# Band attention's values as one pair of weight blocks with seven products, its weight sums written in place

## The reference, cut to what matters

```python
def chunk_band_attention(h, w_qkv, q_g, k_g, rel_bias):
    qkv = (h @ w_qkv).reshape(bsz, seq, 3, C_HEADS, C_HEAD_DIM)
    q = rmsnorm(qkv[:, :, 0], q_g) * (C_HEAD_DIM ** -0.5)
    k = rmsnorm(qkv[:, :, 1], k_g)
    v = qkv[:, :, 2]
    ...
        s = jnp.einsum('bqhd,bkhd->bhqk', q_c, k_b).astype(jnp.float32) + bias
        s = jnp.where(valid, s, -jnp.inf)
        prob = jax.nn.softmax(s, -1).astype(v.dtype)
        return jnp.einsum('bhqk,bkhd->bqhd', prob, v_b)
```

## Time and profile before

| what | value |
|---|---|
| time, median of 3 runs | 2069.96 us (2067.13 to 2071.61) |
| the profiled execution | 2068.74 us, its span 2067.0 us |
| TensorE busy | 2025.5 us, 98% of the span |
| VectorE busy | 1172.6 us, 57% |
| ScalarE busy | 403.8 us, 20% |
| mean granted TensorE clock | 0.993 of full speed |

### The profile page before, as it was taken

One profiled execution on the slowest core, in us unless ns is written; L12 is line 12 of the kernel. 1 busy time (PEld: TensorE's weight loads), 2 busy tenths in 40 slices (PEclk: granted clock), 3 DMA queues, 4 the chain that ended last, 5 costly groups with the idle time before them and its releaser, 6 DMA issues.

```text
span 2067.0 us, 24997 instructions
## 1 busy us (share of the span) xinstructions
PE 2025.5 (98%) x10844; PEld 1439.1 (70%) x10844; DVE 1172.6 (57%) x1651; ACT 403.8 (20%) x831; POOL 10.7 (1%) x22
## 2 busy tenths in 40 slices
PE   8999999999999999999999999999999999999998
PEld 7886766984486599446864556988884466659973
DVE  4664784754463475544434854455555674636776
ACT  3313111000122401103112642111110112321110
POOL 0000000000000000000000000000000000000000
PEclk9999999999999999999999999999999999999999
DMA  5535785445353244433232002122223443124442
GB/s 204 210 117 210 290 356 210 163 179 208 122 204 123 87 180 177 183 143 127 82 122 82 1 0 82 70 94 86 102 97 150 193 171 143 41 82 154 173 156 88
DMA packets 22749, 292.68 MB, mean 142 GB/s; under 512 B 2752, under 2 KB 3008, under 8 KB 4848
## 3 DMA queue, kind: packets, MB, share of 16 engines
q1 hardware_dynamic: 20864, 280.67, 35.7%
q0 software_dynamic: 1776, 10.43, 1.4%
HBM read 290.03 MB, written 1.05 MB: 141 GB/s over the span
## 4 chain that ended last, share of the span: by engine, by line
PE 90%; DVE 7%; DMA 2%; ACT 1%; issue 0%; SPq 0%; DVEq 0%; ACTq 0%
PE bank L325 88%; DMA ring<-in_W 2%; PE bank L686 1%; DVE small L855 1%; DVE arena L876 1%; PE bank L779 0%; DVE arena L697 0%; DVE arena L640 0%; DVE arena L850 0%; ACT arena L813 0%; DVE arena L869 0%; DVE ADR L1047 0%; DVE arena L2652 0%; ACT arena L695 0%; DVE HT L697 0%
## 5 line engine op out<-in xcount | busy, mean ns | idle before, releaser
L325 PE MATMUL bank<-arena 128*128 128x128 f32 (+10 forms) x3840 | 672.3, 349 | 7.4 <-DVE arena L1708 2.1
L325 PEld LDWEIGHTS bank<-arena 128*128 128x128 f32 (+4 forms) x3840 | 472.1, 184 | 189.8 <-issue 148.0
L325 PE MATMUL bank<-HT,ring 128*128 128x128 f32 (+1 forms) x2448 | 408.5, 325 | 2.5 <-DMA ring<-in_W 2.0
L325 PEld LDWEIGHTS bank<-HT,ring 128*128 128x128 f32 x2448 | 363.8, 192 | 42.7 <-issue 9.8
L325 PE MATMUL bank<-ring,arena 128*128 128x512 f32 (+1 forms) x674 | 295.4, 593 | 0.6 <-ACT arena L695 0.6
L325 PEld LDWEIGHTS bank<-ring,arena 128*128 128x128 f32 (+1 forms) x674 | 126.8, 190 | 156.1 <-issue 155.5
L325 PE MATMUL bank<-ring,HT 128*128 128x512 f32 (+2 forms) x512 | 193.2, 534 | 1.0 <-ACT HT L2020 0.8
L325 PE MATMUL bank<-arena,ring 128*128 128x128 f32 (+4 forms) x1158 | 187.2, 322 | 0.1
L325 PEld LDWEIGHTS bank<-arena,ring 128*128 128x128 f32 (+3 forms) x1158 | 165.4, 189 | 15.3 <-issue 2.2
L325 PEld LDWEIGHTS bank<-ring,HT 128*128 128x128 f32 x512 | 89.6, 192 | 98.5 <-issue 95.4
L695 ACT ACTIVATE arena<-bank 128x512 f32<-128x512 f32 (+2 forms) x126 | 69.0, 573 | 445.7 <-PE bank L325 442.3
(11 more groups left out here) (307 smaller groups left out, 1556.4 us busy)
## 6 DMA issues: line engine op xcount, KB each, us to landing
ring<-in_W SPq DMA_DIRECT2D x125, 2048.0 KB, 7.9
ring<-in_W SPq DMA_DIRECT2D x6, 1536.0 KB, 8.8
ring<-in_W SPq DMA_DIRECT2D x4, 1024.0 KB, 9.0
arena<-in_rel POOLq DMA_DIRECT2D x1, 2048.0 KB, 10.9
arena<-in_rpb POOLq DMA_DIRECT2D x1, 2048.0 KB, 9.1
arena<-in_dft POOLq DMA_DIRECT2D x2, 640.0 KB, 6.5
X<-in_x SPq DMA_DIRECT2D x2, 512.0 KB, 5.6
X<-in_ctx POOLq DMA_DIRECT2D x1, 1024.0 KB, 5.1
```

The source lines that it names most:

```text
L325: return nc.tensor.matmul(out_, lhsT, rhs, start=start, stop=stop, skip_group_check=True)
```

## The change

The values become one pair (`qkv4`, `qkv5`) with seven products of 4 matmuls 128x512, with the tokens as the stationary side (`pe_band_values`). The token sums `QKT` of q and k serve again. Of the four weight sums one goes to `QKS[0][0]`, and three are written over quarters of the two ring slots (`dve_band_sums`). `qkv4` and `qkv5` join `SUMMED`. The banks are named: x, z, w, y get 0, 1, 2, 3; k's norm sum gets 4 and its spread 4 to 7. v1.1 and its copy no longer stand inside the attention; k's norm sum now follows product 5 and its spread product 6. VectorE makes sums 5 and 7 in front of the k pair's `dve_seven_u`, and puts the values together instead of ScalarE.

```diff
+        def pe_band_values(between):
+            A11, A12, A21, A22 = band_quarters()
+            into = {1: "x", 5: "z", 7: "w", 2: "x", 6: "y", 3: "z", 4: "w"}
+            for j in (1, 5, 7, 2, 6, 3, 4):
+                if j in (1, 5):
+                    weight("qkv4" if j == 1 else "qkv5")
+                if j in (1, 5, 7, 6):
+                    bank[into[j]] = open_bank(f"bvals {into[j]}0", "xzwy".index(into[j]))
+                w = {1: A11, 5: QKS[0][0], 7: A21, 2: A12, 6: A11, 3: A12, 4: A22}[j]
+                x = {1: HT[:, 0:4, 0:P], 2: HT[:, 4:8, 0:P], 3: HT[:, 4:8, P:SEQ], 5: QKT[0], 6: QKT[1], 7: QKT[2], 4: QKT[3]}[j]
+                if j in (5, 7, 6, 3):
+                    pe.wait_ge(vector_done, at(f"bvals sum.{j}"))
+                if j == 2:
+                    pe.wait_ge(scalar_done, at("bvals m1 out0"))
+                if j == 3:
+                    pe.wait_ge(scalar_done, at("bvals m5 out0"))
+                if j == 4:
+                    pe.wait_ge(vector_done, at("bvals m7 used0"))
+                for k in range(4):
+                    last = mm(bank[into[j]][:, :], x[:, k, :], w[:, k, :], j in (1, 5, 7, 6) and k == 0, j in (2, 6, 3, 4) and k == 3)
...
+        def dve_band_sums(which):
+            A11, A12, A21, A22 = band_quarters()
+            S1 = QKS[0][0]
+            for x in ("qkv4", "qkv5"):
+                dve.wait_ge(slot_loaded[WAT[x] % RING], 16 * (WAT[x] // RING + 1))
+            for j, d, a, b, op, read in ((5, S1, A21, A22, ALU.add, "k pair p0.5"), (7, A21, A11, A21, ALU.subtract, None),
+                                         (6, A11, S1, A11, ALU.subtract, "bvals p0.1"), (3, A12, A12, A11, ALU.subtract, "bvals p0.2")):
+                if j in which:
+                    if read:
+                        dve.wait_ge(tensor_done, at(read))
+                    dve.wait_ge(vector_done, dve.n)
+                    tt(d, a, b, op).then_inc(vector_done, dve.one())
...
             # TensorE
-            values(0)
+            def k_sum():
+                state["bank"] = 4
+                pe_norm_sum("k3", [(g % 4, (g // 4) * SEQ, SQK3[:, g, :]) for g in range(8)])
+            def k_spread():
+                state["bank"] = 4
+                pe_norm_spread("k3", INV3[:, 1, :])
+            pe_band_values({5: k_sum, 6: k_spread})
             pe.wait_ge(vector_done, at("k3 normed"))
-            pe_pairs("band", band_steps, PB3, {1: lambda: values(1, 7), 2: lambda: pe.wait_ge(scalar_done, at("v out"))})
+            pe_pairs("band", band_steps, PB3, {2: lambda: pe.wait_ge(vector_done, at("v out"))})
             # ScalarE
+            act_seven_copy("bvals", 0, 1, QM1)
+            act_seven_copy("bvals", 0, 5, QM5)
             act_norm_root("k3", INV3[:, 1, :])
-            for t in range(2):
-                copy_out(act, f"v0.{t}", VB[:, t, 0:512])
-            copy_out(act, "v1.0", VB[:, 0, 512:1024])
+            ps = full(act, "bvals x0")
+            activation(VB[:, 0, 0:512], ps[:, :], ACT.Copy).then_inc(scalar_done, act.one())
             # VectorE
                 if n == "k":
                     normed(0, "q3", QB)
+                    dve_band_sums((5, 7))
                 dve_seven_u(l, 0, QM1)
...
+            dve_band_sums((6,))
             dve_norm_inverse("k3", INV3[:, 1, :])
+            dve_band_sums((3,))
+            dve_seven_q("bvals", 0, QM5)
             normed(1, "k3", KB)
+            dve_seven_u("bvals", 0, QM1)
+            dve_seven_c("bvals", 0, "z", VB[:, 1, 0:512], QM1, lambda v: v)
+            dve_seven_c("bvals", 0, "w", VB[:, 0, 512:1024], QM1, lambda v: v)
+            tt(VB[:, 1, 512:1024], QM1, QM5, ALU.add).then_inc(vector_done, dve.one())
+            dve.wait_ge(scalar_done, at("read bvals x0"))
+            dve.mark("v out")
```

More of the change, by code:

```diff
@@ L284, in build @@
         WAT = {name: i for i, (name, _) in enumerate(PLAN)}
-        SUMMED = {name for name, _ in PLAN if name.startswith(("down", "up", "cdown")) or name in ("qkv0", "qkv1", "qkv2", "qkv3","win3", "win4", "win0", "win1") or name.startswith("cup") and not name.endswith(".0")}
+        SUMMED = {name for name, _ in PLAN if name.startswith(("down", "up", "cdown")) or name in ("qkv0", "qkv1", "qkv2", "qkv3", "qkv4", "qkv5","win3", "win4", "win0", "win1") or name.startswith("cup") and not name.endswith(".0")}
         def at(name):
@@ L2249, in build, with band_quarters @@
         QKT = [arena[:, ar.at - 3840 + 512 * j:ar.at - 3328 + 512 * j].rearrange("p (k c) -> p k c", c=P) for j in range(4)]
+        def band_quarters():
+            a, b = (ring[:, WAT[x] % RING, :].rearrange("p (k c) -> p k c", k=KT) for x in ("qkv4", "qkv5"))
+            return a[:, 0:4], a[:, 4:8], b[:, 0:4], b[:, 4:8]
+        def pe_band_values(between):
+            A11, A12, A21, A22 = band_quarters()
+            into = {1: "x", 5: "z", 7: "w", 2: "x", 6: "y", 3: "z", 4: "w"}
+            bank = {}
+            for j in (1, 5, 7, 2, 6, 3, 4):
[15 more added lines that the diff above has]
+                    last = mm(bank[into[j]][:, :], x[:, k, :], w[:, k, :], j in (1, 5, 7, 6) and k == 0, j in (2, 6, 3, 4) and k == 3)
+                last.then_inc(tensor_done, pe.one())
+                pe.mark(f"bvals p0.{j}")
+                if j in (3, 4):
+                    pe.mark(f"slot of {'qkv4' if j == 3 else 'qkv5'}")
+                if j in (2, 3, 4, 6):
+                    marks[f"bvals {into[j]}0"] = marks[f"bvals p0.{j}"]
+                if j in between:
+                    between[j]()
@@ new lines, in dve_band_sums @@
+        def dve_band_sums(which):
[10 more added lines that the diff above has]
+                    tt(d, a, b, op).then_inc(vector_done, dve.one())
+                    dve.mark(f"bvals sum.{j}")
+            if which[-1] == 3:
+                dve.mark("summed qkv4", "summed qkv5")
@@ L2278, in pe_attn @@
                                    (0, 6): lambda: pe_norm_spread("q3", INV3[:, 0, :])})
-            w = weight("qkv4").rearrange("p (k c) -> p k c", k=KT)
-            for t in range(2):
[L2281 to L2302, removed]
-            values(0)
+            def k_sum():
[5 more added lines that the diff above has]
+            pe_band_values({5: k_sum, 6: k_spread})
             pe.wait_ge(vector_done, at("k3 normed"))
-            pe_pairs("band", band_steps, PB3, {1: lambda: values(1, 7), 2: lambda: pe.wait_ge(scalar_done, at("v out"))})
+            pe_pairs("band", band_steps, PB3, {2: lambda: pe.wait_ge(vector_done, at("v out"))})
             def band_out(k, t):
@@ L2329, in act_attn @@
                 act.mark(f"{n}3 sq")
+            act_seven_copy("bvals", 0, 1, QM1)
+            act_seven_copy("bvals", 0, 5, QM5)
             act_norm_root("k3", INV3[:, 1, :])
-            for t in range(2):
-                copy_out(act, f"v0.{t}", VB[:, t, 0:512])
-            copy_out(act, "v1.0", VB[:, 0, 512:1024])
[L2335 to L2339, removed]
+            ps = full(act, "bvals x0")
+            activation(VB[:, 0, 0:512], ps[:, :], ACT.Copy).then_inc(scalar_done, act.one())
+            act.mark("read bvals x0")
+            act_pairs("band", band_steps, PB3)
         def dve_attn():
```

## The result

The change made the kernel **0.32% slower**: ratio 1.0032, 95% interval 1.0024 to 1.0040, from 11 runs of each (median 2076.64 us against 2069.35), which is 6.6 us, with 5.0 to 8.3. The profiled execution took 2076.64 us, with a span of 2074.8.

The account below looks back on a forecast made before the run. TensorE, busy 98%, bounds the kernel. 3.4 waiting less 3.85 products plus 4.1 lost cover gives 3.7; clock adds 1.7 and 0.4: 5.8, or 4.7 with median landing. Taken 5.5 over 2069.96: 2075.5 us, range 2070.5 to 2080.

Parts of the forecast that it names:

- Products removed: Values on TensorE: 32 matmuls become 28, 64 passes become 56, taking 3.85 us off its work.
- The wait in front of product 1: TensorE idles 3.4 us for bank 0, because sums 5 and 7 run on VectorE before z is read.
- the profiled landing: Load of `qkv5` landing 9.0 us after issue, as profiled; gives a 3.4 us wait at product 1.
- the median one: Load of `qkv5` landing at the median 7.9 us; gives a 2.3 us wait at product 1.
- The other waits: Sums 6 and 3, squares, reciprocal and `aout1`'s load are covered: cost nothing, at most 2.3 us each if uncovered.
- The lost cover: Attention start without v1.1: L850 of step 2 stands 6.6 us behind the scores' start, 4.1 us in the sum.
- The clock: Granted clock drops behind both TensorE gaps: 1.7 us behind the first, 0.4 behind the second, in the attention.
- The sum: Whole change: 5.8 us with the profiled landing, 4.7 with the median one; 5.5 taken.
- the first: Rival 1, both gaps: waits come but the clock holds; +2.6 to +3.7 us, 2073.1 us; chance 0.17.
- the second: Rival 2, product 1: bank wait has no price, z bank read early enough; 2070.3 us, no change; chance 0.07.
- third: Rival 3, round 2 of attention: softmax doesn't hold it up, products pay in full; 2066.1 us, faster; chance 0.05.
- The fourth: Rival 4, attention's first rounds: slow clock lasts two stretches more, each 1.7 us; 2078.9 us; chance 0.09.

Follow-up runs that it names:

- sums_late: Changed kernel with sums 5 and 7 moved behind the k pair's z addition; ratio 1.0003 to the kernel before, stage 57.87 us.
- fill_stall: Changed kernel with ten unread 128x128 matmuls on TensorE in front of product 1; ratio 1.0027 to the kernel before, stage 61.22 us.
- before_two_sums: Kernel before plus two unread 128x2048 sums on VectorE where the change put sums 5 and 7; ratio 1.0020, stage 61.63 us.
- old_ahead: Kernel before with v1.1 and its copy moved out of the attention to stand ahead of it; ratio 1.0030, stage 62.48 us.
- fill_both: Changed kernel with ten unread matmuls before product 1 and nine before the first transposes; ratio 1.0012 to the kernel before, stage 60.53 us.
- old_ahead_look: Kernel before with v1.1 moved ahead of the attention, run once more unaltered for a second profile; stage 61.68 us, no ratio.
- split_cover: Changed kernel with sums 5 and 7 behind the z addition, products 3 and 4 inside the attention, banks moved; ratio 0.9973 to the kernel before, stage 54.23 us.

## Why the prediction was right

The direction, the mechanisms and the place were right, and the time lies in the range. By its steps:

- **Products removed.** At full clock the seven products with both norm parts take 26.60 us (sums_late), 24.53 without the norm parts; the prediction had 24.30, from the earlier trace rows. The gain is 3.6 instead of 3.85.
- **The wait in front of product 1.** Forecast 3.4 with the profiled landing and 2.3 with the median one; measured 2.50, 2.80 and 2.68 in the three profiles of the changed kernel, with landings of 8.3, 8.6 and 8.5 us. The forecast counted from the moment where v0.0 would have started, 3.57 us behind the start of the k pair's last product; so counted they are 2.67, 2.97 and 2.85. The mechanism is right and the size hangs on the landing: fill_stall had the 9.0 and with it 3.35, counted the same way. From the first sum's start to product 1 it took 6.09 us, forecast 6.1. before_two_sums shows the wait to be a cause by itself, sums_late shows that without it the loss is gone.
- **The other waits.** Sums 6 and 3, the squares, the reciprocal and the load of `aout1` hold nobody: between product 1 and the scores TensorE has no gap. (The forecast's 656.8 for the end of product 2 is a slip of 0.6: by its own durations, 642.5 + 4 x 3.47 + 1.00, it is 657.4. Nothing hangs on it.)
- **The lost cover.** L850 of step 2 stands 6.35 us behind the scores (forecast 6.6), which makes the lost cover 3.9 us where the sum had 4.1. TensorE's idle time has a piece that the prediction left out, 0.88 us in front of step 2's scores, which wait until L850 of step 0 has read their banks; it lies inside the same 6.35 and adds nothing. old_ahead shows the step by itself.
- **The clock.** Drops behind both gaps, as forecast. The first costs 1.7 us (forecast 1.7), shown by product 1's 5.37 against 3.67 with fillers. The second costs 0.1 in the changed kernel's profile and 0.3 to 0.4 by the two pairs with and without fillers; the forecast took 0.4. "Three gaps of this size, three drops" was true of that one trace; over all thirteen profiles the same three gaps have a drop behind them in 33 of 39 cases. In the stage all eleven gaps of 2.46 us and more have one. The Trainium skill's rule in "TensorE: Matmul & The Clock Gate", its part on the clock gate, that idleness throttles the array to half its rate, agrees with the traces of the stage: a lower clock follows each of these gaps, and none follows the filled ones.
- **The sum.** The stage lost 4.8 to 5.1 us in three profiles, against 5.5 forecast. The timed ratio says 6.6, with 5.0 as its lower end. What the stage doesn't hold, 1.5 to 1.8 us at the middle, isn't settled, so that the time lies above the forecast and the stage below it; that 5.5 comes so near to the time is in part luck. The mean granted clock points one way: 0.9915 against 0.9938 is 0.0023 x 2070 = 4.8 us of lost work more, where the two drops in the profile make 3.4. Whether some timed executions have a doubled second drop, as old_ahead's profiles did, or lose more ahead of the stage, no profile here shows.

Of the rivals, the first (the clock holds) fell to the windows, the second and third to the gap and to the 6.35 us. The fourth, a slow clock through the first rounds, didn't come in the changed kernel's three profiles; old_ahead had something like it, with 3.4 us of work lost, of which it paid 1.8 and 1.0 us.

## What to carry to other kernels

When work is added to an engine that is idle most of the time, ask which buffers its later instructions free: here 4.6 us of sums, on an engine that is busy 57% of the time, stood in front of the read that freed a bank, and cost more than the removed matmuls were worth. A block that fills TensorE's time at the start of a pipeline, where the first steps wait for each other, has a worth beyond its own work: v1.1, 7.07 us long, saved 3.5 us by its place alone (old_ahead). If it must change its form, keep some of it in that place. A short idle gap on a dense TensorE is to be priced with the clock drop behind it, which here added two thirds to the first gap's cost.

## What the runs showed of the hardware

- What the same kind of drop costs depends on where it falls: 1.7 us in front of dense 128x512 matmuls, 0.1 in the changed kernel's first attention rounds, but 1.8 and 1.0 behind the same kind of gap in old_ahead's two profiles, where the windows show 3.4 us of work lost instead of 1.7.
- Whether a gap is followed by a drop can differ between executions. The three gaps of the earlier trace rows, 2.14 to 2.64 us in the thirteen profiles, lost 1.7 us of work or nothing: in fill_stall and before_two_sums the first is followed by a clock of 1.00, in fill_both and old_ahead_look the second, in old_ahead and split_cover the third. How much of the scatter of the times comes from this isn't shown.
- Two executions of the kernel before reached the same instruction 3.5 us apart (635.57 and 639.03), while the densely occupied stage behind it repeated within 0.01 us. A difference of a few microseconds in one profile's span says little until it is placed.
- The load of `qkv5`, 2 MB issued from the same place in the program, landed after 8.3 to 9.1 us in the thirteen profiles. Where the sums stood in front of the bank's read, the spread came through as waiting: 2.50 us with a landing of 8.3, 2.68 with 8.5, 2.80 with 8.6 (the changed kernel's three profiles).
